# Two token halves skewed over the borders between eight stages of a two-block kernel

## What is computed

```python
x = layer_norm(ALPHA * x + g1 * mixer(modulate(x, sh1, sc1)))      # stage 0: indexer attention and convolution
x = layer_norm(ALPHA * x + g2 * swiglu(modulate(x, sh2, sc2)))     # stage 1: 1024 -> 2816 -> 1024
x = x + gate * sublayer(modulate(rms_norm(x), shift, scale))       # stages 2 to 7:
# 2 SwiGLU, 3 differential attention, 4 and 5 SwiGLU, 6 HGRN2 (gated linear recurrence in chunks), 7 SwiGLU
```

## Time and profile before

| what | before |
|---|---|
| median of 3 runs | 1599.02 us (1597.28 to 1599.33) |
| span of the profiled execution | 1598.3 us (the page has no other time of it) |
| TensorE busy | 1431.5 us, 90% |
| VectorE busy | 1088.6 us, 68% |
| ScalarE busy | 668.1 us, 42% |
| GpSimd busy | 177.5 us, 11% |
| chain that ended last, by engine | TensorE 73%, VectorE 16%, ScalarE 4%, DMA 3% |

### The profile page before, as it was taken

The page is one execution under the profiler, slowest core; times in us unless marked ns, Lnnn a source line. Parts: engine busy times, 40 slices in busy tenths (PEclk is TensorE's granted clock), DMA queues, the critical chain, the costliest instruction groups (busy, mean ns, idle before and its releaser), DMA issues.

```text
span 1598.3 us, 19161 instructions
## 1 busy us (share of the span) xinstructions
PE 1431.5 (90%) x6855; PEld 1189.2 (74%) x6855; DVE 1088.6 (68%) x1058; ACT 668.1 (42%) x747; POOL 177.5 (11%) x271
## 2 busy tenths in 40 slices
PE   1876769999799999996899999999998798899998
PEld 1775557888678888774678888788888787778886
DVE  4678774777658886657467775678866698555554
ACT  0433224444254434544353444534446744344442
POOL 1101220111121110210011110211101000100000
PEclk9887778999889999995789999999999899889999
DMA  7741644999468994550168995689954433066671
GB/s 298 259 167 46 229 148 158 310 322 322 155 234 307 342 337 172 185 184 0 53 211 269 315 312 179 223 279 355 336 201 132 146 117 105 27 197 210 211 231 71
DMA packets 183523, 333.96 MB, mean 209 GB/s; under 512 B 8634, under 2 KB 122911, under 8 KB 182322
## 3 DMA queue, kind: packets, MB, share of 16 engines
q1 hardware_dynamic: 157040, 237.95, 44.4%
q0 software_dynamic: 26112, 95.07, 16.6%
q10 hardware_dynamic: 322, 0.27, 0.1%
HBM read 330.64 MB, written 2.62 MB: 209 GB/s over the span
## 4 chain that ended last, share of the span: by engine, by line
PE 73%; DVE 16%; ACT 4%; DMA 3%; issue 2%; POOL 1%; ACTq 0%; DVEq 0%; POOLq 0%
PE ps L1462 67%; DVE wlo L878 2%; DMA ada_raw<-in_w_ada 2%; PE ps L1580 2%; DVE ada_acc L1401 1%; POOL st L415 1%; DVE ada_acc L1027 1%; PE ps L1534 1%; ACT xn L562 1%; DVE xn L943 1%; PE ps L1515 1%; ACT xn L565 1%; DVE ada_acc L897 1%; PE ps L1665 1%; PE ps L1608 1%
## 5 line engine op out<-in xcount | busy, mean ns | idle before, releaser
L878 DVE TENSOR_TENSOR wlo<-raw,whi 128x2048 fp32r<-128x2048 f32 x215 | 490.2, 2285 | 166.0 <-ACT whi L525 166.0
L525 ACT ACTIVATE whi<-raw 128x2048 fp32r<-128x2048 f32 x215 | 409.7, 1909 | 264.1 <-PE ps L1462 241.7
L1462 PE MATMUL ps<-whi,hhi 128*128 128x512 f32 (+1 forms) x1208 | 486.5, 403 | 22.5 <-DVE wlo L878 7.9
L1462 PE MATMUL ps<-wlo,hhi 128*128 128x512 f32 (+1 forms) x1208 | 476.3, 394 | 0.0
L1462 PE MATMUL ps<-whi,hlo 128*128 128x512 f32 (+1 forms) x1208 | 476.2, 394 | 0.0
L1462 PEld LDWEIGHTS ps<-whi,hhi 128*128 128x128 f32 x1208 | 231.2, 191 | 76.5 <-issue 15.7
L1462 PEld LDWEIGHTS ps<-whi,hlo 128*128 128x128 f32 x1208 | 230.7, 191 | 49.3
L1462 PEld LDWEIGHTS ps<-wlo,hhi 128*128 128x128 f32 x1208 | 231.2, 191 | 47.4 <-issue 1.4
L897 DVE SCALAR_TENSOR_TENSOR ada_acc<-ada_raw,csil,ada_acc 128x1024 f32<-128x1024 f32 x120 | 150.4, 1278 | 12.7 <-DMA ada_raw<-in_w_ada 10.3
L1462 PE MATMUL ps<-whi,ahi 128*128 128x512 f32 x400 | 156.1, 390 | 0.0
L1462 PE MATMUL ps<-whi,alo 128*128 128x512 f32 x400 | 155.7, 389 | 0.0
(11 more groups left out here) (233 smaller groups left out, 1387.8 us busy)
## 6 DMA issues: line engine op xcount, KB each, us to landing
raw<-in_ffn_w_in SPq DMA_DIRECT2D x176, 512.0 KB
ada_raw<-in_ada_w POOLq DMA_DIRECT2D x96, 512.0 KB, 5.3
raw<-in_ffn_w_down SPq DMA_DIRECT2D x44, 1024.0 KB
big<-in_ada_w POOLq DMA_DIRECT2D x48, 512.0 KB, 6.7
ada_raw<-in_w_ada POOLq DMA_DIRECT2D x32, 512.0 KB, 4.6
raw<-in_hgrn_w_in SPq DMA_DIRECT2D x16, 1024.0 KB
raw<-in_attn_w_qkv SPq DMA_DIRECT2D x12, 1024.0 KB
raw<-in_w_gate SPq DMA_DIRECT2D x22, 512.0 KB
```

The source lines that it names most:

```text
L525: sc.activation(whi[:, slot, 0:n], raw[:, slot, 0:n], ACT.Copy).then_inc(w_hi, 1)
L878: ve.tensor_tensor(wlo[:, slot, 0:n], raw[:, slot, 0:n], whi[:, slot, 0:n].bitcast(F32), ALU.subtract)\
L1462: done = pe.matmul(dst, lhsT, rhs, start=first and n == 0, stop=final and n == 2, skip_group_check=True)
```

## The change

At each border the two halves of the tokens are set against each other. `close` runs the last two units by half: both units for t0, then the column sums, then t1 of the first of them, the transposes of t0, t1 of the second. `enter` starts the next stage with t0 of its first unit, the gate sum, the transposes of t1, t0 of the second unit, and then t1 of both. `gated`, the residual, the moments, the norm and the scaling go by 512 columns, each with a count of its own (`y_ready` three times and `x_new` four times in a stage). VectorE's `conclude` and ScalarE's `leave` hold the new order of their part. The last chunk of a SwiGLU is turned and split by half. The column sums move from bank 5 to bank 7. Stage 6 takes the first value block ahead of the two forget blocks, so that its first units can go by half too; the query blocks go to banks 4 to 7, and six value and gate units instead of eight stand beside levels 0 to 4 (`HGRN_BESIDE`). The output goes out in four transfers instead of two, and TensorE's loop of two over attention's first blocks is written out.

```diff
-COL_BANK = 5
-HGRN_BLOCKS = (1024, 1536, 0, 512, 2048, 2560, 3072, 3584)
+RMS_ROOT = {1: 6, 2: 9, 3: 21, 4: 23, 5: 25, 6: 29}
+COL_BANK = 7
+HGRN_BLOCKS = (2048, 1024, 1536, 0, 512, 2560, 3072, 3584)
+HGRN_BESIDE = ((0, 1), (2,), (3,), (4,), (5,), (), (), (), ())
...
+            def square(s, t, h):
+                sc.wait_ge(x_new, 4 * s + 2 * t + h + 1)
+                cols = slice(h * BANK, (h + 1) * BANK)
+                part = 250 * h + 1 + 2 * t
+                sc.activation(xn[:, t, cols], xs[:, t, cols], ACT.Square, scale=1.0 / 32,
+                              accum_out=st[:, part:part + 1]).then_inc(sums_s, 1)
+            def scaled(s, t):
+                sc.wait_ge(root, root_count(RMS_ROOT, s, t))
+                for h in range(2):
+                    cols = slice(h * BANK, (h + 1) * BANK)
+                    sc.activation(xn[:, t, cols], xs[:, t, cols], ACT.Copy, scale=st[:, 1 + 2 * t:2 + 2 * t]).then_inc(h_src, 1)
+            def leave(s):
+                n = s + 1
+                if s:
+                    for h in range(2):
+                        square(s, 0, h)
+                    scaled(s, 0)
+                sc.wait_ge(cols_set, n + 1)
+                modulate(n, 0)
+                if s > 1:
+                    square(s, 1, 0)
+                hi(FIRST[n] + 1)
+                if s == 1:
+                    square(s, 1, 0)
+                if s:
+                    square(s, 1, 1)
+                    scaled(s, 1)
+                modulate(n, 1)
+                if n not in LATE_GATES:
+                    set_gate(n)
...
+            def gated(s, t, h):
+                if t and h:
+                    ve.wait_ge(w_used, used(FIRST[s + 1] - 1))
+                else:
+                    ve.wait_ge(y_ready, 3 * s + 2 * t + h + 1)
+                cols = slice(h * BANK, (h + 1) * BANK)
+                link(ve.tensor_tensor(xn[:, t, cols], bank(2 * t + h), gate[:, s % 2, cols], ALU.mult))
+                return xs[:, t, cols], xn[:, t, cols]
+            def residual(s, t, h):
+                x_h, y_h = gated(s, t, h)
+                ve.tensor_tensor(x_h, x_h, y_h, ALU.add).then_inc(x_new, 1)
+            def moments(s, t):
+                stats = st[:, 12 + 12 * t:24 + 12 * t]
+                for h in range(2):
+                    x_h, y_h = gated(s, t, h)
+                    link(ve.scalar_tensor_tensor(x_h, x_h, ALPHA, y_h, ALU.mult, ALU.add))
+                    link(ve.bn_stats(stats[:, 6 * h:6 * h + 6], x_h))
+                ve.bn_aggr(st[:, 4 + 2 * t:6 + 2 * t], stats).then_inc(sums_v, 1)
...
+            def conclude(s):
+                n = s + 1
                 ve.wait_ge(gate_set, s + 1)
+                if s == NSUB - 1:
                     for t in range(NT):
+                        for h in range(2):
+                            residual(s, t, h)
                     return
+                if s < 2:
+                    moments(s, 0)
+                    lo(FIRST[n])
+                    layer_norm(s, 0)
+                else:
+                    residual(s, 0, 0)
+                    residual(s, 0, 1)
+                    lo(FIRST[n])
+                set_columns(n)
+                ve.wait_ge(cols_set, n + 1)
+                modulate(n, 0)
+                if s < 2:
+                    rest_of_input(n, 0, 0)
+                    rest_of_input(n, 0, 1)
+                    moments(s, 1)
+                    lo(FIRST[n] + 1)
+                    layer_norm(s, 1)
+                else:
+                    residual(s, 1, 0)
+                    rest_of_input(n, 0, 0)
+                    residual(s, 1, 1)
+                    rest_of_input(n, 0, 1)
+                    lo(FIRST[n] + 1)
+                modulate(n, 1)
+                rest_of_input(n, 1, 0)
+                rest_of_input(n, 1, 1)
...
-                body(U + 3 * (NCH - 1) - 1, NCH - 1, more=False)
+                lo(U + UNITS[s] - 2)
+                alo_of(NCH - 2)
+                multiply(NCH - 1, 0)
                 lo(U + UNITS[s] - 1)
-                alo_of(NCH - 1, final=True)
+                multiply(NCH - 1, 1)
+                alo_last(0)
+                alo_last(1)
                 conclude(s)
...
+                for j in range(2, 6):
+                    lo(U + j)
...
-                lo(U + 9)
-                lo(U + 10)
+                lo(U + 11)
+                lo(U + 12)
                 for level in range(len(LEVELS) + 2):
                     if level:
                         decay(level)
                         take_scores(level - 1)
                         if level <= len(LEVELS):
                             differences(level + 1)
-                    if level <= 7:
-                        lo(U + 11 + level)
+                    for n in HGRN_BESIDE[level]:
+                        lo(U + 13 + n)
...
+            def enter(s, banks, ready):
+                unit = FIRST[s]
+                if s - 1 in LATE_GATES:
+                    pe.wait_ge(gate_set, s)
+                columns_of(unit, 0, 0, banks[0], inputs=s)
+                if s not in LATE_GATES:
+                    sum_gate(s)
+                if s > 2:
+                    transpose_inputs(s, 1)
+                columns_of(unit + 1, 1, 0, banks[0], inputs=s).then_inc(ready, 1)
+                if s <= 2:
+                    transpose_inputs(s, 1)
+                for g in range(2):
+                    columns_of(unit + g, g, 1, banks[1], inputs=s).then_inc(w_used, 1)
...
+            def close(s, one, two, before_one, before_two):
+                before_one(0)
+                rows_of(*one, 0, False, False)
+                before_two()
+                rows_of(*two, 0, False, True, signal=y_ready).then_inc(y_ready, 1)
+                if 0 < s < NSUB - 1:
+                    sum_columns(s + 1)
+                before_one(1)
+                rows_of(*one, 1, False, False).then_inc(w_used, 1)
+                if 1 < s < NSUB - 1:
+                    transpose_inputs(s + 1, 0)
+                rows_of(*two, 1, False, True, signal=y_ready).then_inc(w_used, 1)
+                if s == 0:
+                    sum_columns(1)
+                if s < 2:
+                    transpose_inputs(s + 1, 0)
...
-                    pe.wait_ge(h_lo, 4 * 6 + 3 + g)
-                    columns_by_feature(U + g, g, 0)
-                for g in range(2):
-                    columns_by_feature(U + 2 + g, g, 2)
+                enter(6, (4, 5), blk_ready)
                 for b in range(2):
-                    pe.wait_ge(f_taken, b + 1)
                     for g in range(2):
-                        columns_by_feature(U + 4 + 2 * b + g, g, 2 * b)
+                        columns_by_feature(U + 2 + 2 * b + g, g, 2 * b)
+                for b in range(2):
+                    if b == 0:
+                        pe.wait_ge(vg_out, 2)
+                    else:
+                        pe.wait_ge(gate_set, 7)
+                    for g in range(2):
+                        columns_by_feature(U + 6 + 2 * b + g, g, 4 + 2 * b)
```

More of the change, by code:

```diff
@@ L586, in body @@
                     ahi_of(i - 1)
-                    if more:
-                        hi(first + 3, lap)
+                    hi(first + 3, lap)
                     silu(i, first + 1, lap)
@@ L794, in _ @@
             hi(U)
-            split_inputs(0)
+            sc.wait_ge(cols_set, 1)
+            for t in range(NT):
+                modulate(0, t)
             hi(U + 1)
@@ L996, in body @@
+                def body(first, i, lap=0, kt=None):
                     pieces = range(count) if kt is not None else ()
@@ L1494, in columns_by_feature, with rows_of, down_rows @@
                 done.then_inc(w_used, 1)
-            def down_rows(unit, hi_of, lo_of, first, final, lap=0, before=None, end=None):
+            def rows_of(unit, hi_of, lo_of, t, first, final, lap=0, signal=None):
                 slot = unit % RING
-                pe.wait_ge(w_lo, unit + 1 + RING * lap)
+                if t == 0:
+                    pe.wait_ge(w_lo, unit + 1 + RING * lap)
+                for h in range(2):
+                    for k in range(2):
+                        cols = slice(k * D + h * BANK, k * D + (h + 1) * BANK)
+                        done = three(bank(2 * t + h), hi_of(k, t), lo_of(k, t), whi[:, slot, cols], wlo[:, slot, cols],
+                                     first and k == 0, final and k == 1)
+                    if signal and h == 0:
+                        done.then_inc(signal, 1)
+                return done
+            def down_rows(unit, hi_of, lo_of, first, lap=0, before=None):
                 for t in range(NT):
@@ L1565, in swiglu, with gate_up @@
+                close(s, place(2), place(3), lambda t: mixed(2, t), lambda: None)
             def swiglu(s):
-                m = SWIGLUS.index(s) * NCH
+                m, turned = SWIGLUS.index(s) * NCH, SWIGLUS.index(s) * (NCH + 1)
                 U = FIRST[s]
```

(12 more changed lines are left out.)

403 lines of the change are left out of this document (188 added, 215 removed).

## The result

The changed kernel takes 1611.03 us in the median (1609.65 to 1615.54, 4 runs), the kernel before 1598.77 beside it. The ratio is 1.0079, 95% interval 1.0059 to 1.0100: slower by 0.8%, where 1600.0 and a range of 1591 to 1607 had been predicted. The profiled execution spans 1609.5 us instead of 1598.3.

The account below looks back on a forecast made before the run. TensorE, 90% busy, was taken as the bound, with time to win where it stops at stage borders. Terms +0.8 +1.6 -1.2 -2.4 -2.7 -2.6 +8.6 -1.2 gave +0.9: 1599.2 us profiled, 1600.0 in the median; range 1591 to 1607.

Parts of the forecast that it names:

- first part of the plain borders: Border steps for the first token half: TensorE's column sums and 12 products hidden, stage entered 11.35 us after the border's zero.
- plain borders: Stage borders without layer norm: predicted gains 1.2 in 2→3, 2.4 in 3→4, 2.7 in 4→5, 2.6 in 6→7; 8.9 us.
- layer norm borders: Borders 0→1 and 1→2: second half's moments come behind the first half's lo copies; losses of 0.8 and 1.6 us.
- Rival (c): Slower because TensorE's clock falls ahead of the second half's products: 1605.1 us, or 1613 in a larger form; chance 0.19.
- the fall ahead of t1's products: In 3→4, 6→7 and 0→1, clock 0.50 when the second half's products start: 1.7 us each, 1605.1 us.
- the smaller form: Clock falls only ahead of the second half's products, not behind the column sums: 1605.1 us; chance 0.19 covers both forms.
- 11.35: Plain borders: us from VectorE taking the first half's second block until TensorE enters the next stage, after idling 1.0.
- The held root: At the borders, GpSimd's root waits for VectorE's lo copy to end; unheld, the total would be 9.6 us less.
- Rival (a): At the borders, lo copies don't hold GpSimd's root: 9.6 us less in all, 1590.4 us; chance 0.13.
- Stage 6: Value block ahead of forget blocks delays the bounding forget path, levels win nothing: loss of 8.6 us.
- rival (b): Stage 6 pays nothing, since the value block fills TensorE's stops: 1591.4 us; chance 0.17.
- (d): The halves wait for each other, so plain borders keep their length: about 1609 us; chance 0.11, shared with mishaps.

## Why the prediction was wrong

**The step that failed** is in the first part of the plain borders: "TensorE has column sums to 3.5 and 12 products to 6.4 meanwhile: hidden." The 12 products were priced at full speed right behind the run of 1-column products. In four of the five plain borders the clock fell there, and they ended, counted from VectorE's second product with the gate, at 9.3 in 2→3, 9.1 in 6→7, 7.7 in 4→5 and 7.6 in 5→6, so 1.2 to 2.9 later than that; the run of sums itself took up to 4.74, where it takes 3.63 at full clock. With the sums spread, which alone takes that away, the kernel ran at 1600.10, the forecast's 1600.0. That is partly luck: of what remained, the layer norm borders were 3.8 worse than predicted and the plain borders as much better.

Rival (c) named this: "If it also fell behind the column sums in five borders, 1613." It fell in four, for 9.7 us together. What (c) put first, the fall ahead of t1's products, came true in 0→1, for a few products in 6→7, and not in 3→4. The mechanism and its price were there; the chance of 0.19, shared with the smaller form, was too low, and the range ended at 1607 with this case at 1613. The trace of the kernel before could have told more. The earlier trace rows has the clock at 1.00 through the column sums of 3→4 and at 0.50 when the products come, and I took the first as an answer about what follows directly. The stretch between the two, and the transposes that start 0.70 behind the sums:

```profile
802.50:806.00 3.50, 2.05 (x9) 0.52 0.23 57
...
803.28 1.97 PE L1515 MATMUL ps<-kc,xn 128*128 128x128 f32 x8 [0.70 <-ACT xn L565]
```

In the borders 2→3 to 6→7 of that trace the 3.5 us behind the sums had a granted clock of 0.65, 0.52, 0.75, 0.68 and 0.59. TensorE was idle for part of each, so they don't prove that busy products would be slow there; but they are no ground for full speed.

**Plain borders.** In an undisturbed clock the mechanism gave more than I said. With the sums spread VectorE takes the first half's second block at 992.17 and the stage's first product stands at 1002.85: 10.7, where I had 11.35. The idle 0.84 ahead of it (1.0 predicted) and 1.07 ahead of the second half's transposes (1.1) are in the trace. By the steps of the table less the clock, the four plain borders give 2.7, 4.1, 3.5 and 2.4: 12.7 instead of 8.9 (the first two only as a sum). That 3→4 seems to give most may be in part that its products ran at half clock before; this was not tested.

**The held root** was right as a fact and wrong as a price. The lo copy held it 1.3 us in the first half too, and no time hung on it. It was GpSimd's first step that waited, not the power, which changes nothing in the sum. Rival (a) read a free power of 0.54 in the earlier trace rows, but the same rows have one of 1.52 at 1000.42. It ran beside VectorE's addition of two SBUF tensors (L963, 1000.30 to 1001.53), so an addition seems to hold a root as a lo copy does.

**The layer norm borders** were undersized: +6.2 for +2.4. I counted VectorE's serial order, and in 1→2 the half clock of the second half's products (1.8), but took the transposes at full speed: they took 1.87 and 1.97 where they take 1.03 to 1.27 at full clock, and both stand on the path. In 0→1 I counted no half clock at all, and the second half's first 14 products had it. The run with VectorE's order changed shows that 3.25 us of 1→2 were a choice of order, and with spread sums as well 6.1. What is left at 0→1 stays open: from stage 0's first product with the gate to stage 1's the changed kernel took 217.8 us, and the kernel with stage 6 in its old order, whose code is the same there, 215.1.

**Stage 6** was right in its mechanism: rival (b), that it pays nothing, is refuted, and moving the forget path back is worth 6.8 us, 1.5 of them by the clock. The size was off by 2.8: 1.65 is the clock in its border, 1.6 the attended values at half clock. They ran so in every traced kernel with the new order and not with the old one, and the prediction has no term for it.

**Rivals.** (a) falls with the held roots in the rows, and the freed root that gained nothing. (d) falls with the 34 us of the entry that isn't skewed.

## What to carry to other kernels

When a change moves large products from ahead of a run of one-column products to behind it, price them at both clocks, even if the engine is busy throughout: the busy share of a stretch doesn't tell the clock of the next one. Interleaving the small products with the large ones cost nothing here and was worth 0.7%; where no large product followed the run it made the kernel slower. And a skew of halves needs a start that can use one half: where the first block that matters needs both (stage 6), keep the old order and pull the second half forward instead.

## What the runs showed of the hardware

A run of sixteen 128x1 products, in which TensorE is busy in every us, can bring the granted clock from 1.00 to half: 0.73 and 0.58 over the 10 us from 635 on, with the 12 products behind it at 4.9 us for 2.7. The same run left it at 1.00 in 3→4, and in 1→2 of the changed kernel; in 1→2 of the kernel with VectorE's order changed it fell to 0.72 and 0.60, with the same sums and products there. No run here tells what decides it. Split into four, with three products of 512 columns between, it lowered the clock behind them in none of the five plain borders.
